# A two-block network in one launch: the first projection is the values', row by row, with loads in order of use

## What is computed

```python
def rmsnorm(x, g):
    xf = x.astype(jnp.float32)
    var = jnp.mean(xf * xf, axis=-1, keepdims=True)
    return (xf * lax.rsqrt(var + EPS) * g.astype(jnp.float32)).astype(x.dtype)

def mixer_sublayer(x, ln1_g, w_in, ...):
    h = rmsnorm(x, ln1_g)
    proj = h @ w_in
    q_sb, k_sb, v_sb, q_hg, f_hg, i_hg, g_hg, gate_sb, gate_hg = jnp.split(proj, splits, axis=-1)
    ...
    y_sb = stick_breaking_attention(sb_heads(q_sb), sb_heads(k_sb), sb_heads(v_sb))
    ...
```

## Time and profile before

| what | us |
|---|---|
| median of 3 runs | 1679.96 |
| lowest and highest of them | 1678.16, 1684.01 |
| the profiled execution | 1681.17 |
| its span (first to last instruction) | 1679.4 |

### The profile page before, as it was taken

How to read it: one execution, slowest core, us unless ns; L and a number is a source line. 1 busy time by engine, 2 the same in 40 slices (tenths; PEclk the granted TensorE clock), 3 DMA queues, 4 the chain that set the end, 5 groups by cost and what they waited for, 6 DMA issues and landing times.

```text
span 1679.4 us, 19749 instructions
## 1 busy us (share of the span) xinstructions
PE 1610.6 (96%) x7736; PEld 1279.9 (76%) x7736; DVE 1056.2 (63%) x1773; ACT 809.2 (48%) x1350; POOL 199.8 (12%) x274
## 2 busy tenths in 40 slices
PE   6999999999999999999979999999999899999999
PEld 5866667777788788888867766877767788888887
DVE  3356995777647898989967687565664333333321
ACT  5366665322445688888855443323332533333221
POOL 0000003332123400000024111110100000000000
PEclk8999999999999999999999999999999899999999
DMA  5312112101544899999972121012112222232322
GB/s 186 98 59 70 51 51 76 51 26 51 166 175 151 233 386 421 422 421 422 377 274 76 51 100 51 26 53 98 51 51 75 76 93 87 96 100 87 102 101 88
DMA packets 78627, 236.28 MB, mean 141 GB/s; under 512 B 6944, under 2 KB 9280, under 8 KB 66240
## 3 DMA queue, kind: packets, MB, share of 16 engines
q1 hardware_dynamic: 67264, 204.49, 33.9%
q10 hardware_dynamic: 7632, 18.37, 2.9%
q0 software_dynamic: 3632, 12.08, 1.9%
HBM read 222.33 MB, written 12.60 MB: 140 GB/s over the span
## 4 chain that ended last, share of the span: by engine, by line
PE 80%; DVE 12%; ACT 4%; issue 1%; POOL 1%; DMA 1%; ACTq 0%; DVEq 0%; POOLq 0%
PE bank L98 77%; PE bank L101 3%; DVE low L123 2%; DVE REST L113 2%; ACT REST L104 1%; DVE REST L123 1%; DVE REST L126 1%; ACT CHH L107 1%; DVE AL L113 1%; DVE low L113 1%; DVE REST L119 1%; DVE REST L132 1%; ACT AH L107 1%; ACT REST L107 1%; DVE st L129 0%
## 5 line engine op out<-in xcount | busy, mean ns | idle before, releaser
L113 DVE TENSOR_TENSOR low<-slot,CHH 128x1024 fp32r<-128x1024 f32 (+1 forms) x300 | 297.3, 1033 | 113.3 <-ACT CHH L107 112.3
L107 ACT ACTIVATE CHH<-slot 128x1024 fp32r<-128x1024 f32 (+1 forms) x300 | 259.1, 901 | 135.0 <-PE bank L98 58.1
L123 DVE SCALAR_TENSOR_TENSOR low<-slot,smalls,CHH 128x512 fp32r<-128x512 f32 (+1 forms) x232 | 169.9, 762 | 210.6 <-ACT CHH L107 210.4
L98 PE MATMUL bank<-AH,CHH 128*128 128x512 f32 x608 | 246.9, 406 | 4.7 <-DVE low L123 2.8
L98 PE MATMUL bank<-AL,CHH 128*128 128x512 f32 x608 | 239.1, 393 | 0.0
L98 PE MATMUL bank<-AH,low 128*128 128x512 f32 x608 | 238.9, 393 | 0.0
L107 ACT ACTIVATE CHH<-slot,smalls 128x512 fp32r<-128x512 f32 (+1 forms) x232 | 154.9, 701 | 169.2 <-PE bank L98 74.7
L98 PE MATMUL bank<-CHH,AH 128*128 128x512 f32 x512 | 216.1, 422 | 4.0 <-DVE low L123 1.8
L98 PE MATMUL bank<-low,AH 128*128 128x512 f32 x512 | 200.7, 392 | 0.0
L98 PE MATMUL bank<-CHH,AL 128*128 128x512 f32 x512 | 200.2, 391 | 0.0
L98 PE MATMUL bank<-REST 64*128 64x128 f32 (+6 forms) x1200 | 172.4, 307 | 14.0 <-DVE REST L113 4.4
(11 more groups left out here) (169 smaller groups left out, 2388.9 us busy)
## 6 DMA issues: line engine op xcount, KB each, us to landing
slot<-in_w_in SPq DMA_DIRECT2D x36, 1024.0 KB, 5.2
slot<-in_w_exp_gate SPq DMA_DIRECT2D x32, 1024.0 KB, 13.4
slot<-in_w_exp_up SPq DMA_DIRECT2D x32, 1024.0 KB, 14.0
slot<-in_w_exp_down SPq DMA_DIRECT2D x32, 1024.0 KB, 14.1
slot<-in_w_gate SPq DMA_DIRECT2D x10, 1024.0 KB, 5.1
slot<-in_w_up SPq DMA_DIRECT2D x10, 1024.0 KB, 5.1
slot<-in_w_down SPq DMA_DIRECT2D x10, 1024.0 KB, 5.0
slot<-in_w_out SPq DMA_DIRECT2D x8, 1024.0 KB, 5.2
```

Source lines behind the costliest of these rows:

```text
L98: return self.e.matmul(out, l, r, start=start, stop=stop) if self.e else Issued()
L107: return self.e.activation(out, in_, ACT.Copy, scale=scale) if self.e else Issued()
L113: return self.e.tensor_tensor(out, a, b, op) if self.e else Issued()
L123: return self.e.scalar_tensor_tensor(out=out, in0=a, scalar=s, in1=b, op0=op0, op1=op1) if self.e else Issued()
```

## The change

The first segment is `v_sb`, with its rows outside, in slots 0 and 1; then `q_sb` in slots 2 and 5, `k_sb` in 0 and 1, and the others go round 2, 0, 1. SyncE issues the blocks of tokens and the weights without a wait between, in the order of use; the first slot is loaded in two halves (the semaphore `w_first` stands for the first half). Constants, masks and `lamb` come after the first four slots. The first two blocks of tokens are not copied scaled and transposed: VectorE scales two identity matrices by the norm (`diag`), and TensorE multiplies the raw tokens by them. Blocks 2 and 3 are scaled by VectorE instead of ScalarE and transposed between steps 12 and 13 and between 17 and 18 of `v_sb`. The turning uses banks 4 to 7. Before all that TensorE runs 14 matmuls of a matrix of ones, whose result is not used. The table for exponentials is loaded at ScalarE's start.

```diff
+FIRST_TURN = 12, 17
+WARM = 14
...
-    for n, (name, feat) in enumerate((("q_sb", 1), ("k_sb", 1), ("v_sb", 0), ("q_hg", 1), ("f_hg", 1), ("v_hg", 0),
-                                      ("g_hg", 0), ("gs0", 1), ("gs1", 1), ("gh0", 1), ("gh1", 1))):
-        plan_seg(name, w_in, 512 * n, feat, gain=sc("ln1"))
+    first_turns = {"v_sb": (0, 1), "q_sb": (2, 5), "k_sb": (0, 1)}
+    in_turn = itertools.cycle((2, 0, 1))
+    for n, (name, feat) in zip((2, 0, 1, *range(3, 11)), (
+            ("v_sb", 0), ("q_sb", 1), ("k_sb", 1), ("q_hg", 1), ("f_hg", 1), ("v_hg", 0), ("g_hg", 0),
+            ("gs0", 1), ("gs1", 1), ("gh0", 1), ("gh1", 1))):
+        plan_seg(name, w_in, 512 * n, feat, gain=sc("ln1"), turns=first_turns.get(name))
...
+        def turn_scaled(i):
+            for half in range(2):
+                b, old = banks.use("n1", ("n1", i, half))
+                pe.wait_ge(*at(("x", i)))
+                pe.wait_ge(*at(("n1", "c", i)))
+                pe.wait_ge(*at(old))
+                for k in range(4):
+                    m = pe.matmul(cols(b, k), cols(x3[:, i, :], 4 * half + k), diag[i], True, True)
+                m.then_inc(*mark("pe_turned", ("n1", "t", i, half)))
...
+        for _ in range(WARM):
+            pe.matmul(psum[7][:, 0:P], ones, ones, True, True)
         pe.wait_ge(*at("ident"))
-        for i in range(NT):
-            turn("n1", i, scratch1.buf(("cp", "n1", i)), ("n1", "c", i), ("cp", "n1", i))
+        turn_scaled(0)
+        turn_scaled(1)
+        beside = dict(zip(FIRST_TURN, (lambda: turn_first(2), lambda: turn_first(3))))
+        n = 0
+        for _ in seg("v_sb", hT, lambda k, j: ("n1", "lo", j, k // 4), rows=True):
+            n += 1
+            if n in beside:
+                beside[n]()
         drain(seg("q_sb", hT, all_of("n1")))
         drain(seg("k_sb", hT, all_of("n1")))
-        drain(seg("v_sb", hT, rows_of("n1")))
...
+        squares("n1", 0, x3[:, 0, :], scratch1, ss0, ("x", 0))
+        squares("n1", 1, x3[:, 1, :], scratch1, ss0, ("x", 1))
+        split_chunks(v0)
+        hi_of("n1", 0, 0, hT[0])
+        split_chunks(v0 + 1)
+        hi_of("n1", 0, 1, hT[0])
+        split_chunks(v0 + 3)
+        hi_of("n1", 1, 0, hT[0])
+        hi_of("n1", 1, 1, hT[0])
+        split_chunks(v0 + 7)
+        squares("n1", 2, x3[:, 2, :], scratch1, ss0, ("x", 2))
+        squares("n1", 3, x3[:, 3, :], scratch1, ss0, ("x", 3))
...
-            if s.number < 3:
-                for i in range(NT):
-                    sp.wait_ge(*at(("x", i)))
-            sp.dma_start(s.ap, s.src).then_inc(sem(f"w_land{s.i}"), 16)
+            if s.number == 0:
+                sp.dma_start(s.ap[:, 0:2, :], s.src[:, 0:2, :]).then_inc(sem("w_first"), 16)
+                sp.dma_start(s.ap[:, 2:4, :], s.src[:, 2:4, :]).then_inc(sem(f"w_land{s.i}"), 16)
+            else:
+                sp.dma_start(s.ap, s.src).then_inc(sem(f"w_land{s.i}"), 16)
+            if s.number == 1:
+                load_rows(2)
+                load_rows(3)
```

More of the change, by code:

```diff
@@ L398, in _build @@
     psum = [ctx.enter_context(nc.psum_tensor(f"bank{i}", [P, 512], F32))[:, :] for i in range(8)]
-    banks = Banks(psum, {"main": (0, 1, 2, 3), "zp": (4, 5), "tp": (6,), "op": (7,), "four": (0, 1, 2, 3), "three": (0, 1, 2), "row": (3,), "all": tuple(range(8))})
+    banks = Banks(psum, {"main": (0, 1, 2, 3), "zp": (4, 5), "tp": (6,), "op": (7,), "four": (0, 1, 2, 3), "three": (0, 1, 2), "n1": (4, 5, 6, 7), "row": (3,), "all": tuple(range(8))})
     rings = []
@@ L473, in plan_seg @@
             src = w[(k0 + k) * P:(k0 + k + m) * P, n0:n0 + n].rearrange("(k p) n -> p k n", p=P)
-            s = plan_slot(turns[k // 4] if turns else next(in_turn) if part == 3 else len(slots) % 3, src, m, n, part)
+            s = plan_slot(turns[k // 4] if turns else next(in_turn), src, m, n, part)
             for q in range(s.nk):
@@ L529, in _build, with landed @@
         plan_seg(f"wd{n}", t["w_down_2"][0], 512 * n, 0, nk=FT, part=3)
+    def landed(c):
+        s, q = CH[c]
+        return (sem("w_first"), 16) if s.number == 0 and q < 2 else (sem(f"w_land{s.i}"), s.landed)
     def raw(c):
@@ L2007, in vector, with scaled_first @@
         dve.tt(gains, sc("fin"), sc("nmix"), ALU.mult).then_inc(*mark("dve_own", "gains"))
-        norm_turn(N1)
+        def scaled_first(i, dst, src):
+            dve.wait_ge(*at(("n1", "rs", i)))
+            dve.ts(dst, src, r0[:, i:i + 1], None, ALU.mult).then_inc(*mark("dve_norm", ("n1", "c", i)))
+        v0 = SEG["v_sb"][0]
+        dve.wait_ge(*at("ident"))
+        scaled_first(0, diag[0], ident)
+        scaled_first(1, diag[1], ident)
+        split_chunks(v0)
+        lo_of("n1", 0, 0, hT)
+        split_chunks(v0 + 1)
+        lo_of("n1", 0, 1, hT)
+        split_chunks(v0 + 3)
+        lo_of("n1", 1, 0, hT)
+        lo_of("n1", 1, 1, hT)
+        split_chunks(v0 + 7)
+        for i in (2, 3):
+            scaled_first(i, scratch1.buf(("cp", "n1", i)), x3[:, i, :])
+        n = 0
+        for _ in seg("v_sb", rows=True):
+            n += 1
+            for i in (2, 3):
+                if n == FIRST_TURN[i - 2] + 1:
+                    for half in range(2):
+                        lo_of("n1", i, half, hT)
         dve.wait_ge(*at("consts"))
@@ L2972, in sync, with load_rows @@
     def sync(sp):
+        def load_rows(i):
+            sp.dma_start(x3[:, i, :], xd[:, i, :]).then_inc(*mark(f"d_row{i}", ("x", i), by=16))
+        load_rows(0)
+        load_rows(1)
+        late = {4, 5, 6, 7}
         for s in slots:
@@ L2975, in sync @@
                 sp.wait_ge(sem("slot_free"), s.former.number + 1)
-            elif s.i in (4, 5, 6, 7):
+            if s.i in late and s.number > 3:
+                late.remove(s.i)
                 sp.wait_ge(*at(("y2", 3)))
@@ L2979, in sync @@
                     sp.wait_ge(*at("x again"))
-            elif s.i == 3:
+            elif s.i == 3 and s.former is None:
                 for i in range(2, NT):
```

38 lines of the change are left out of this document (23 added, 15 removed).

## The result

| | median us | lowest, highest | runs |
|---|---|---|---|
| the kernel before, beside it | 1679.06 | 1677.22, 1684.01 | 4 |
| the changed kernel | 1668.28 | 1667.41, 1669.16 | 4 |

The ratio is 0.9919, with a 95% interval of 0.9903 to 0.9936: faster, by 11 to 16 us. A repeat gave 1668.13 and 0.9923 (0.9907 to 0.9940). The profiled execution took 1668.18 us, 13.0 less than that of the kernel before; its span is 1666.2.

A forecast was written before the change was run, and what follows sets the result against it. TensorE was taken as the bound, dense only from 22.26 us. First row to 18.1, plus 16.3, 2.2 and 43.5, puts the 289th matmul at 80.1, not 90.50: gain 10.4, 1670.8, less 1.2 is 1669.6 us; range 1666 to 1674.5.

The forecast's parts named there:

- Everything later: All work behind the first three segments keeps its order, so the start's gain of 10.4 us should reach the end.
- The 1.2 us off for the profiled execution: The profiled 1681.17 us stood 1.2 above the median, so the forecast was lowered from 1670.8 to 1669.6.
- Loads: SyncE's first loads land in order: block 0 at 4.4 us, block 1 at 7.0, slot 0's halves at 8.25 and 9.5.
- Scales: Norm scale and scaled identity at the start: ready at 6.8 us for block 0, 9.4 for block 1.
- VectorE's chain: In `v_sb`'s first row, VectorE's 7.96 us of work from 9.4 to 17.4 sets the pace, not TensorE.
- Rest of `v_sb`: After the first row, 24 steps take 16.3 us and 16 transposes 2.2; the segment ends at 36.6.
- Start of attention: VectorE's later `k_sb` copies and ScalarE's saved work come out about level where attention begins; costed at nothing.
- The warm-up: TensorE's 14 matmuls of ones at the start, over by 7.0 us, are covered by block 0's scale wait; costed at nothing.
- Slots: Weights for `q_sb` (slots 2, 5) land by about 18 to 20 us, `k_sb`'s by 42, before its start at 58.
- rival 1: TensorE's clock falls in the first row's gaps, 11 to 18 us, losing 3 us: gain 7.4, 1672.6 us; chance 0.15.
- Rival 2: The first loads share bandwidth and land out of order, at 18 us: no gain, 1680.7 us; chance 0.06.
- Rival 3: Moved slot loads of `q_hg` to `bh1` come late, 6.7 us idle each; three make 1689.7 us; chance 0.04.

The follow-up runs named there:

- copied_turn: The changed kernel with blocks 0 and 1 scaled into a copy by VectorE and transposed, in place of the scaled identities; 1668.16 us.
- no_warm: The changed kernel without the 14 matmuls of ones at TensorE's start; 1675.90 us.
- three_slots: The changed kernel without slot 5, so that `q_sb`'s second half goes to slot 0 behind `v_sb`'s use of it; 1672.45 us.
- turn_all_first: The changed kernel with all four blocks of tokens turned ahead of the first dense matmul, as before; 1676.87 us.
- loads_only: The kernel before with only its loads changed: SyncE issues them without a wait, all four blocks of tokens first, order of work kept; 1679.88 us.

## Where the prediction failed, and where it was right

The mechanism was right and the size was not: I forecast 10.4 us, and it is 13.0 between the two profiled executions and 13.6 by the ratio (0.9919 of 1681). Three terms of the sum failed.

- **Loads and transposes.** I put block 1's landing at 7.0 us; it landed at 6.13, and VectorE's chain began at 8.43 instead of 9.4. I put the transposes of blocks 2 and 3 at 1.09 us each; they took 0.79. By this the 289th matmul came 1.3 us earlier than forecast, at 78.8 instead of 80.1.
- **Everything later, at nothing.** I let the start's gain reach the end at its own size. The part behind the scores took 1.5 us less than in the trace that I had read, and 4.1 less than in the other trace of before. Why stays open (below).
- **The 1.2 us off for the profiled execution.** I took it for 1.2 above the kernel's usual time, by three runs. The later medians, 1681.3 to 1683.4, show that it was usual and the three runs were low.

That my 1669.6 lies only 1.3 from the measured 1668.28 is in part luck: the 1.2 that I took off wrongly and the 1.5 that I left out nearly cancel. So is the size at the start: before's loss to the low clock was 2.9 us in one execution and 1.7 in the other, so the start's gain is 11.7 against one trace of before and 9.9 against the other, and 10.4 lies between.

One by one:

- **What bounds the kernel, and that the start is the place: right.** The start gave 9.9 to 11.7 of the 13 us.
- **Loads: the mechanism right, a term mis-sized.** Where the trace shows a landing of SyncE's twelve loads, nine of them, it is in the order of issue: 4.6, 6.1, 7.5, 12.8, 14.1, 19.5, 22.5, 23.7 and 24.0. I put block 1 at 7.0, the middle between 5.6 and 8.3; it landed at 6.13, nearer the full queue's spacing. The first half of slot 0 was there at 7.51, not 8.25. Block 0 came at 4.65, not 4.4.
- **Scales.** From block 1's landing to the scaled identity I had 2.4 us; it took 2.39 (6.13 to 8.52). So the duration was right, and VectorE's chain began at 8.43 instead of 9.4 by the landing alone. That error carried through.
- **VectorE's chain: right.** It sets the first row's pace, 7.77 us against 7.96, and TensorE's next row began at 17.19 instead of 18.1, 0.9 early. `copied_turn` shows it: a chain 0.7 us later, scores 0.7 later. But TensorE is close behind it, which I had not seen: in `no_warm` its turning ended 1.8 us later, and the scores came 1.3 later.
- **Rest of `v_sb`: right but for the transposes**, which took 0.79 each from first to next matmul (19.92 to 20.71), where I had 1.09: 0.6 less for two. `q_sb` began at 35.30, not 36.6, and the 289th matmul at 78.8, not 80.1.
- **The size against before: too small.** Of the 2.6 us between 10.4 and 13.0, 1.3 are the start's, and 1.5 lie behind the scores (1586.1 us from there to the end of the span before, 1584.6 after), less 0.2 outside the span.
- **What is open.** The part from the scores to the end took 1586.1 and 1588.7 in two traces of before, 1584.6, 1583.4 and 1584.7 in three of the changed kernel, at the same work. No single place holds the difference; pieces between landmarks differ by 1 to 3 us even between traces of one kernel, with the granted clock. I have not found what sets it, nor why the changed kernel should be better there.
- **Start of attention, at nothing: right.** TensorE had no idle time from 20 to 80, and none between the last dense matmul and the scores; VectorE's copies ended at 79.7, and ScalarE's first exponential ran at 80.48.
- **The warm-up, at nothing: right for its cover, wrong for its worth.** It ended at 6.3, 0.93 ahead of the first scale. I priced the failure to warm at 3 us, by rival 1; at the start it was 1.3. But I had no thought of the matmuls as 56 places in a program; without them the wait at the branch, far behind, is 6 us longer.
- **Slots: right.** `q_sb`'s second half in slot 5 had slack, but only there: without that slot the kernel takes 4.3 more.
- **Rival 1 (the clock falls in the trickle): did not come.** TensorE's only listed wait in the first row was 0.54 us, and the stretch 0 to 20 shows 1.00. That figure alone says little, for it is 1.00 in `no_warm` too, where the turning took 5.62 us; but the matmuls of the row's end stand 0.23 apart, as at the full clock. In `three_slots` a gap of 1.79 was again followed by a mean of 0.66, as in the earlier trace rows. The 1.28 that I gave a step at the low clock is what the trace of before shows at 0.50, 22.83 to 24.11.
- **Rival 2 (loads out of order): refuted** by the landing times above, and in `turn_all_first`, where all twelve loads landed in the order of issue, from 4.7 to 23.0. The same holds for every landing of SyncE's first loads that these traces show. The 2.9 us in this rival's sum are the low clock at before's start: the 16th dense matmul began 6.32 us behind the first, where 15 spacings of 0.227 are 3.40; in the other trace of before the loss was 1.7.
- **Rival 3 (late slot loads, slower): did not come** in the changed kernel, but its mechanism is real: `three_slots` is it, with one late load, at 4.3 instead of the 6.7 that I gave it.

## What to carry to other kernels

Early loads and a row order that can start on the first block belong together: without the first the change kept 7.6 of its 13.6 us, without the second 4.4, and early loads alone on the old order left the time where it was, since ScalarE's queue ended last. Take a kernel's usual time from more than three runs before the profiled execution is set against it. And when dummy instructions or any others are added or removed, compare the longest "issue" waits at branches before believing a mechanism: leaving out 14 matmuls at the start moved such a wait by 6 us here, nearly half of the whole change.

## What the runs showed of the hardware

- Instructions come by DMA: the queue that I take for TensorE's brings 1.03 MB in 63 packets of 16 KB, and its share of the 16 engines' time, 1.0% during the wait of the changed kernel, stands beside the 66.5% of the largest data queue there. At a branch under full DMA load (391 to 408 GB/s where read) TensorE waited 6.4 to 7.4 us in 15 traces and 12.4 to 12.7 in the three without warm-up matmuls, where two packets came.
- An instruction packet seems to delay data as well: in `no_warm` and its two repeats one fell on the write of the experts' last result, which then landed after 4.0 to 4.5 us. In the 15 other traces none fell on it, and it took 2.6. GpSimd's gathers began 4.8 to 5.2 us behind its issue instead of 3.4.
- Issuing was not free with much queued: behind nine loads SyncE's issue of the constants took 5.25 us, against 0.4 for a single load. In `loads_only`, behind seven, it took 2.66; in `three_slots`, behind eight, 0.53, and the next one 2.19.
- 14 matmuls of 2 columns took no less time than 14 of 128: 6.13 us for the 28 records, against 4.95 to 6.26 in the other kernels. The weight loads of 128 columns that go with them took 6.05 of the 6.13.
